# The last three tiles in front of a norm and the first three behind it, 256 tokens at a time

## The chip, the core and the metric

The kernel runs on one core of a Trainium2 chip. TensorE (PE) multiplies, the vector engine (DVE), the scalar engine (ACT) and GpSimd (POOL) do the elementwise work, SyncE (SP) issues most of the DMAs. Each engine works through its own queue in order and waits on semaphores. The metric is the device time of one execution in microseconds; lower is better.

## What is computed

Two layers over x of 512 tokens by 1024 channels, in float32. Each layer has a mixing part with three attention branches and an MLP, and both are wrapped in two norms:

```python
def rms_norm(x, g):
    return x * rsqrt(mean(x * x, -1) + EPS) * g

def hybrid_layer(x, ...):
    h = rms_norm(x, g_mix_pre)
    proj = h @ w_in          # latents, q, k, v of the branches, gate logits
    o_a, o_b, o_c = mla(...) @ w_o_mla, swa(...) @ w_o_swa, stick_breaking(...) @ w_o_sb
    mixed = gates[0] * o_a + gates[1] * o_b + gates[2] * o_c
    x = x + rms_norm(mixed @ w_out, g_mix_post)
    h = rms_norm(x, g_mlp_pre)
    u = square(relu(h @ w_up))                       # 4096 wide
    return x + rms_norm(u @ w_down, g_mlp_post)
```

## The kernel before

Everything is stored transposed: the 128 partitions are channels, the free axis is the 512 tokens, and x, h and y have 8 tiles of 128 channels each (`KT` = 8). A tile of a projection is one PSUM bank of 128 output channels by 512 tokens. It takes 24 matmuls: 8 blocks of the contraction, and for each three products (`three`, L470 to L476), because a float32 value a is split into `a_hi`, rounded to the matmul's type, and `a_lo`, the rest, and hi x hi, hi x lo and lo x hi are summed.

Weights come as chunks of 128 x 1024 through a ring of four slots (`RING`). SP waits until the chunk that held the slot has been used up and loads into `raw`; ACT rounds it to `w_hi` (`split`, L885 to L891), DVE subtracts to `w_lo` (`split`, L1372 to L1379). All orders are written out by hand, one program for each engine, and a table `ORDER` (from `order`, L32 on) names the tiles in the order in which PE makes them; semaphore counts are derived from it. Tiles take the two banks `proj` in turn.

A norm divides by a value that needs all 1024 channels of a token, so it sits between two rows of tiles. The one with gain `g_mix_post` (`POST`) comes behind the 8 tiles of the projection `out`; `MPOST` comes behind the 8 tiles `down` of the last of four groups (`GROUPS`) of the MLP. In what follows a joint is such a place: twice from `out` to `up`, once from `down` to the latents of the next layer, once from `down` to the output. At a joint, for all 512 tokens:

- ACT copies each `out` bank to y and squares it (L1301 to L1307); DVE gathers the squares into `acc` (`gather`, L1381 to L1393). For `down` DVE adds the bank to y first (L1688). PE sums over the partitions with two float32 matmuls against ones (`norm_sum`, L492 to L496), and then runs 28 matmuls whose result nobody reads (`keep_warm`, L499 to L502).
- ACT makes a first guess of the root with Ln and Exp (`norm_guess`, `guess`), DVE refines it with one Newton step in three instructions (`norm_refine`, `newton`).
- `residual` (L1415 to L1431) then runs over the 8 tiles on DVE: `hf` = y x gain x rstd, x += `hf`, and behind it `next_lo`; ACT makes `h_hi` = x x gain in between (`next_in`). The division of the following pre-norm is not waited for: it is applied later, to outputs, so h is x times its gain only.
- PE takes up h tile by tile: `three_tiles` (L528 to L542) keeps three output tiles open in three banks and adds each block of the contraction to all three when its `h_lo` is ready. It stands behind the joints and at the very start, there with weights that came in four pieces through the ACT queue (`first_low`, `first_high`).

At the start SP issues the vectors, x 0, the positions, a table of 16 columns `trig`, then x 1 to x 7; DVE begins with the angles of the positions and goes on to `w_lo` and `h_lo`.

## Time and profile before

| | |
|---|---|
| median of 3 runs | 1803.26 us (1802.73 to 1804.34) |
| the profiled execution | 1804.78 us, of which the span is 1803.0 us |
| granted TensorE clock, mean | 0.993 of full speed |
| busy shares of the span | PE 98%, DVE 59%, ACT 46%, POOL 8% |
| chain that ended last | PE 87%, DVE 7%, ACT 3%, issue 2%, DMA 1% |
| HBM read | 146.75 MB, 84 GB/s over the span |

The span runs from the first to the last event of the core; the rest of the profiled time lies around it. The busy share of an engine counts an instruction from its start to its end. Matmuls overlap one another, so their durations must not be added up; the distance from one start to the next is what a matmul costs. In the rows, "128x512" is partitions by elements, what stands behind "<-" in square brackets is the work that ended an idle time, and L475 is line 475 of the kernel.

### The profile page before, as it was taken

How to read it: one execution, taken by the hardware profiler on the slowest of the kernel's cores; microseconds unless marked ns; L12 is line 12 of the kernel's file. 1: busy time of each engine (PE TensorE's matmuls, PEld its weight loads, DVE VectorE, ACT ScalarE, POOL GpSimd, SP SyncE). 2: the span in 40 equal slices, each digit the busy share in tenths (PEclk: the TensorE clock that was granted, in tenths of full speed). 3: DMA queues.
4: the chain of work that ended last, by engine and by line, in shares of the span. 5: the costliest groups of instructions: out<-in, count | busy, mean ns of one | idle time of the engine just before them, and what ended most of it. 6: DMA issues, size and time to landing. Idle time of an engine off the chain costs nothing.

```text
span 1803.0 us, 20939 instructions
## 1 busy us (share of the span) xinstructions
PE 1760.2 (98%) x8298; PEld 1447.0 (80%) x8298; DVE 1057.7 (59%) x1378; ACT 827.0 (46%) x1115; POOL 145.5 (8%) x140
## 2 busy tenths in 40 slices
PE   8999999999999999999999999999999999999996
PEld 6888888888878888888778888888888788888884
DVE  6887875654547534354487777665544564344544
ACT  7576655555345413131366755655544353231221
POOL 0111121111100000000001112111111000000000
PEclk8999999999999999999999999999999999999998
DMA  4221112212332222222221221122224132222221
GB/s 149 65 69 67 60 60 70 71 66 75 123 100 90 92 94 99 94 93 94 93 99 62 74 71 48 59 71 71 71 86 138 57 117 94 93 94 94 99 93 66
DMA packets 46609, 152.30 MB, mean 84 GB/s; under 512 B 5296, under 2 KB 7728, under 8 KB 46512
## 3 DMA queue, kind: packets, MB, share of 16 engines
q1 hardware_dynamic: 44784, 147.29, 24.6%
q10 hardware_dynamic: 1728, 3.67, 0.5%
q8 instruction: 66, 1.08, 0.2%
...
HBM read 146.75 MB, written 4.19 MB: 84 GB/s over the span
## 4 chain that ended last, share of the span: by engine, by line
PE 87%; DVE 7%; ACT 3%; issue 2%; DMA 1%; POOL 0%; DVEq 0%; SPq 0%; ACTq 0%
PE bank L475 80%; PE bank L480 4%; PE bank L741 1%; PE bank L701 1%; DVE hf L1422 1%; DVE x L1429 1%; DVE w_lo L1378 1%; DVE h_lo L1411 1%; DMA trig<-in_trig 1%; ACT dn L943 0%; ACT dn L941 0%; ACT w_hi L891 0%; PE bank L551 0%; DVE mx L1472 0%; PE bank L496 0%
## 5 line engine op out<-in xcount | busy, mean ns | idle before, releaser
L475 PE MATMUL bank<-h_hi,w_hi 128*128 128x512 f32 x1248 | 492.2, 394 | 13.2 <-DVE h_lo L1411 11.6
L475 PE MATMUL bank<-h_hi,w_lo 128*128 128x512 f32 x1248 | 487.3, 391 | 0.0
L475 PE MATMUL bank<-h_lo,w_hi 128*128 128x512 f32 x1248 | 487.2, 390 | 0.0
L891 ACT ACTIVATE w_hi<-raw 128x1024 fp32r<-128x1024 f32 (+2 forms) x275 | 277.1, 1013 | 223.4 <-DMA raw<-in_w 222.8
L1378 DVE TENSOR_TENSOR w_lo<-raw,w_hi 128x1024 fp32r<-128x1024 f32 (+2 forms) x275 | 323.9, 1181 | 61.5 <-ACT w_hi L891 55.5
L475 PEld LDWEIGHTS bank<-h_hi,w_hi 128*128 128x128 f32 x1248 | 235.0, 188 | 66.9 <-issue 10.4
L475 PEld LDWEIGHTS bank<-h_hi,w_lo 128*128 128x128 f32 x1248 | 234.9, 188 | 49.8
L475 PEld LDWEIGHTS bank<-h_lo,w_hi 128*128 128x128 f32 x1248 | 235.1, 188 | 48.0 <-issue 1.4
L475 PE MATMUL bank<-u_hi,w_hi 128*128 128x512 f32 x512 | 203.0, 396 | 0.0
L475 PE MATMUL bank<-u_lo,w_hi 128*128 128x512 f32 x512 | 203.0, 396 | 0.0
L475 PE MATMUL bank<-u_hi,w_lo 128*128 128x512 f32 x512 | 203.0, 396 | 0.0
L1688 DVE TENSOR_TENSOR y<-bank,y 128x512 f32<-128x512 f32 x48 | 33.2, 692 | 142.5 <-PE bank L475 142.5
L475 PEld LDWEIGHTS bank<-u_hi,w_lo 128*128 128x128 f32 x512 | 96.4, 188 | 23.5
L475 PEld LDWEIGHTS bank<-u_lo,w_hi 128*128 128x128 f32 x512 | 96.4, 188 | 23.5
L475 PEld LDWEIGHTS bank<-u_hi,w_hi 128*128 128x128 f32 x512 | 96.4, 188 | 23.5
L1667 DVE TENSOR_TENSOR usq<-relu 128x512 f32<-128x512 f32 x64 | 44.3, 691 | 106.0 <-ACT relu L1090 105.4
L1090 ACT ACTIVATE relu<-bank 128x512 f32<-128x512 f32 x48 | 28.6, 595 | 139.2 <-PE bank L475 139.2
L475 PE MATMUL bank<-o_hi,w_hi 128*128 128x512 f32 x192 | 77.4, 403 | 0.0
L475 PE MATMUL bank<-o_hi,w_lo 128*128 128x512 f32 x192 | 76.1, 397 | 0.0
L475 PE MATMUL bank<-o_lo,w_hi 128*128 128x512 f32 x192 | 76.0, 396 | 0.0
L2019 POOL TENSOR_TENSOR mix<-mix,gate 128x512 f32<-128x512 f32 x32 | 44.4, 1391 | 367.8 <-DVE gate L1642 367.8
L1092 ACT ACTIVATE u_hi<-relu 128x512 fp32r<-128x512 f32 x64 | 40.5, 632 | 70.3 <-DVE relu L1662 68.8
...
## 6 DMA issues: line engine op xcount, KB each, us to landing
...
```

The costliest lines, as they stand in the source:

```text
L475: mm = pe.matmul(o, s, m, start=start and i == 0 and j == 0, stop=last and i == n - 1 and j == 2, skip_group_check=True)
L480: return pe.matmul(o, stationary, moving, start=False, stop=True, skip_group_check=True)
L701: mm = pe.matmul(to[:, off + col:off + col + w], a, m, start=off + col == 0 and i == 0, stop=i == 2, skip_group_check=True)
L741: mm = pe.matmul(pv_bank[:, q0:q0 + w], v[:, j, h % 2, :], part[:, s], start=i == 0 and part is p_hi, stop=part is p_lo, skip_group_check= ...
L891: act.activation(w_hi[:, gc % RING, 0:w], raw[:, gc % RING, 0:w], ACT.Copy).then_inc(whi.sem, 1)
L1090: act.activation(relu[:, n % 2, :], tile_bank(name)[:, :], ACT.Relu).then_inc(free_of(name), 1)
L1092: act.activation(u_hi[g % 2][:, t, :], relu[:, n % 2, :], ACT.Square).then_inc(u_h.sem, 1)
L1378: dve.tensor_tensor(w_lo[:, gc % RING, 0:w], raw[:, gc % RING, 0:w], w_hi[:, gc % RING, 0:w].bitcast(F32), ALU.subtract).then_inc(wlo.sem, 1)
L1411: dve.scalar_tensor_tensor(out=h_lo[:, t, :], in0=x[:, t, :], scalar=gain, in1=h_hi[:, t, :].bitcast(F32), op0=ALU.mult, op1=ALU.subtract) ...
L1667: dve.tensor_tensor(usq[:, n % 2, :], relu[:, n % 2, :], relu[:, n % 2, :], ALU.mult)\
L1688: ins = dve.tensor_tensor(y[:, t, :], tile_bank(name)[:, :], y[:, t, :], ALU.add)
L2019: pool.tensor_tensor(mix[:, t, :], mix[:, t, :], gated_at(b, t), ALU.add).then_inc(mix_add.sem, 1)
```

## The change

- `out` and the last group of `down`: tiles 0 to 4 (`HALF` = 5) stay whole. Tiles 5, 6, 7 are made for the first 256 tokens, then 5, 6, 7 again for the other 256 (`halved`). The first half's norm sum is placed in the middle of tile 5's second half, the second half's sum behind the first 9 matmuls of the three tiles that follow (`three_halves`). The second half of tile 7 gets a bank of its own (bank 4).
- The three tiles behind a joint run over all 8 blocks for the first 256 tokens, then for the other 256. `keep_warm` is gone from the joints.
- ACT squares an `out` bank where it lies and copies it to y with the gain applied; for `down` it scales y in place. `residual` therefore no longer multiplies by the gain, and works on two channel tiles of 256 tokens in one instruction. On DVE and ACT the second half's gathers, squares and guess stand between the pairs of the first half.
- The first two weight chunks behind a joint no longer pass through the ring but through two side buffers (`side_raw`, `side_hi`, `side_lo`) that lie over `o_lo` and a part of memory unused at that time.
- At the start positions and `trig` are issued from the ACT queue between the second and the third piece of the first weights; SP issues only the vectors and x before the ring. DVE makes two pieces of `w_lo` and two `h_lo` before it looks at the positions.
- SP stores the result in pairs of tiles, half the tokens at a time.

```diff
-WARM = 28
+HALF = 5
+ALL, HALF_A, HALF_B = slice(0, SEQ), slice(0, SEQ // 2), slice(SEQ // 2, SEQ)
+HALVES = (HALF_A, HALF_B)
...
+    def halved(*name):
+
+        return [e for t in range(HALF) for e in own(*name, t)] \
+            + [((*name, t, h), (*name, t)) for h in range(2) for t in range(HALF, KT)]
+
+    seq += halved("out")
...
-        seq += [e for t in range(KT) for e in own("down", g, t)]
+        seq += [e for t in range(KT) for e in own("down", g, t)] if g + 1 < GROUPS else halved("down", g)
...
+SIDE_CHUNKS = [l * CHUNKS + C[name] for l in range(DEPTH) for name in (("latent", 0), ("latent", 1), ("up", 0, 0), ("up", 0, 1))
+               if l or name[0] == "up"]
+FETCHED = []
+for gc in range(3, DEPTH * CHUNKS):
+    if gc not in SIDE_CHUNKS:
+        FETCHED.append(gc)
+    if gc + KT // 2 in SIDE_CHUNKS:
+        FETCHED.append(gc + KT // 2)
+IN_RING = [gc for gc in range(DEPTH * CHUNKS) if gc not in SIDE_CHUNKS]
+RING_AT = {gc: n for n, gc in enumerate(IN_RING)}
...
+        side_raw = place("side_raw", [P, 2, CH], F32, r1 + 8192)
+        side_lo = place("side_lo", [P, 2, CH], F32R, r1 + 8192)
+        side_hi = place("side_hi", [P, 2, CH], F32R, r1 + 24576)
...
                     sp.dma_start(x[:, t, :], A_x[:, t, :]).then_inc(x_loaded[t], 16)
-                    if t == 0:
-                        sp.dma_start(pos_i[:, :], A_pos.broadcast_to([P, SEQ])).then_inc(angles_loaded, 16)
-                        sp.dma_start(trig[:, :], A_trig).then_inc(angles_loaded, 16)
-                for gc in range(3, DEPTH * CHUNKS):
+                for gc in FETCHED:
                     c = gc % CHUNKS
                     if gc == RING:
                         sp.dma_start(cst_f[:, :], A_const).then_inc(const_loaded, 16)
-                    if gc >= RING:
-                        now[0] = (gc - RING) // CHUNKS
-                        sp.wait_ge(*full(LAST[(gc - RING) % CHUNKS] + 1))
+                    if gc in SIDE_CHUNKS:
+                        now[0] = gc // CHUNKS - (c < C["up", 0, 0])
+                        sp.wait_ge(*full(T[("o", 2, KT - 1) if c >= C["up", 0, 0] else ("down", GROUPS - 2, KT - 1)] + 1))
+                    elif gc >= RING:
+                        gone = IN_RING[RING_AT[gc] - RING]
+                        now[0] = gone // CHUNKS
+                        sp.wait_ge(*full(LAST[gone % CHUNKS] + 1))
...
+                def norm_sum(j, h=0):
+                    e, cols = square_of(j, KT - 1, h)
+                    pe.wait_ge(*summed(SUMMED_AT[j] + gathered(e - 1)))
+                    pe.matmul(sum_bank(h)[:, cols], cst[:, ONE, :].bitcast(F32), acc[:, cols], start=True, stop=False)
+                    pe.wait_ge(*squared(SQUARED_AT[j] + e + 1))
+                    pe.matmul(sum_bank(h)[:, cols], cst[:, ONE, :].bitcast(F32), sq[:, e % 2, cols], start=False, stop=True)\
                       .then_inc(sum_all.sem, 1)
...
+                def halved(name, hi, lo, j, ready=None):
+                    for t, h, one in tiles_of(*name):
+                        tile(one, hi, lo, ready if t == 0 else None,
+                             (lambda: norm_sum(j)) if (t, h) == (HALF, 1) else None, cols_of(t, h))
+                def three_halves(names, ready, j):
+                    def piece(name, t, h):
+                        cols = HALVES[h]
+                        return three(tile_bank(name)[:, cols],
+                                     [(weight(C[name], t), (h_hi[:, t, cols], h_lo[:, t, cols]))],
+                                     start=t == 0 and h == 0, last=t == KT - 1)
                     for name in names:
+                        pe.wait_ge(*wlo(C[name] + 1))
                         take_bank(name)
+                    for h in range(2):
+                        for t in range(KT):
+                            pe.wait_ge(*hlo(ready + KT * h + t + 1))
+                            for name in names:
+                                mm = piece(name, t, h)
+                                if h and t == KT - 1:
+                                    mm.then_inc(full.sem, 1)
+                            if (t, h) == (0, 0):
+                                layer = now[0]
+                                now[0] = layer - (j == MPOST)
+                                norm_sum(j, 1)
+                                now[0] = layer
...
-                    for t in range(KT):
-                        tile(("out", t), mix_hi, mix_lo, (mix_l, 0) if t == 0 else None)
-                    norm_sum(POST)
-                    keep_warm(WARM)
+                    halved(("out",), mix_hi, mix_lo, POST, (mix_l, 0))
 
...
-                    norm_sum(MPOST)
-                    if now[0] + 1 < DEPTH:
-                        keep_warm(WARM)
+                    if now[0] + 1 == DEPTH:
+                        norm_sum(MPOST, 1)
...
+                def out_part(t, h):
+                    name = ("out", t, h) if t >= HALF else ("out", t)
+                    cols = cols_of(t, h)
+                    tile_ready(name)
+                    square(POST, t, tile_bank(name), h)
+                    act.activation(y[:, t, cols], tile_bank(name)[:, cols], ACT.Copy, scale=vec(V_POST + t))\
+                       .then_inc(free_of(name), 1)
+
+                def down_part(t, h):
+                    act.wait_ge(*freed(("down", GROUPS - 1, t, h) if t >= HALF else ("down", GROUPS - 1, t)))
+                    cols = cols_of(t, h)
+                    square(MPOST, t, y[:, t, :], h)
+                    act.activation(y[:, t, cols], y[:, t, cols], ACT.Copy, scale=vec(V_MPOST + t))
...
                     act.dma_start(first(raw, i), A_first[:, 3 * P * a:3 * P * b])\
                        .then_inc(first_loaded[i], 16)
+                    if i == 1:
+                        act.dma_start(pos_i[:, :], A_pos.broadcast_to([P, SEQ])).then_inc(angles_loaded, 16)
+                        act.dma_start(trig[:, :], A_trig).then_inc(angles_loaded, 16)
...
-                        name = ("out", t)
-                        split(C[name] + 2)
-                        tile_ready(name)
-                        act.activation(y[:, t, :], tile_bank(name)[:, :], ACT.Copy).then_inc(free_of(name), 1)
-                        act.wait_ge(*freed(name))
-                        square(POST, t, y[:, t, :])
-                    split(C["up", 0, 2])
+                        if t < HALF:
+                            split(C["out", t] + 2)
+                        if t == HALF - 1:
+                            split(C["out", KT - 1])
+                        out_part(t, 0)
+                        if t == HALF - 1:
+                            split(C["up", 0, 0])
+                        elif t == HALF:
+                            split(C["up", 0, 1])
+                        elif t == HALF + 1:
+                            split(C["up", 0, 2])
                     norm_guess(POST)
+                    out_part(HALF, 1)
                     for t in range(KT):
-                        act.wait_ge(*res(t + 1))
-                        next_in(t, vec(V_MPRE + t))
+                        act.wait_ge(*res(t // 2 + 1))
+                        next_in(t, vec(V_MPRE + t), HALF_A)
+                        if t == 0:
+                            out_part(HALF + 1, 1)
+                        elif t == 3:
+                            out_part(HALF + 2, 1)
+                        elif t == 5:
+                            norm_guess(POST, 1)
...
+                def residual(p, h, n0, then):
+                    cols, n1, pairs = HALVES[h], n0 + KT // 2 * h, KT // 2
+                    def scaled_pair(q):
+                        if q > 1:
+                            dve.wait_ge(*res(n1 + q - 1))
+                        both = rstd[:, cols].unsqueeze(1).broadcast_to([P, 2, SEQ // 2])
+                        dve.tensor_tensor(hf[:, 0:2, HALVES[q % 2]], y[:, 2 * q:2 * q + 2, cols], both, ALU.mult)\
+                           .then_inc(scaled_y.sem, 1)
+                    def added_pair(q):
+                        dve.wait_ge(*scaled_y(n1 + q + 1))
+                        if n0 == 0:
+                            dve.wait_ge(x_loaded[2 * q], 16 * (now[0] + 2))
+                            dve.wait_ge(x_loaded[2 * q + 1], 16 * (now[0] + 2))
+                        to = x[:, 2 * q:2 * q + 2, cols]
+                        dve.tensor_tensor(to, to, hf[:, 0:2, HALVES[q % 2]], ALU.add).then_inc(res.sem, 1)
+                    if p == 0:
+                        scaled_pair(0)
+                        scaled_pair(1)
+                        added_pair(0)
+                        return
+                    if p < pairs:
+                        added_pair(p)
+                    if then:
+                        then(2 * p - 2, h)
+                    if p + 1 < pairs:
+                        scaled_pair(p + 1)
+                    if then:
+                        then(2 * p - 1, h)
...
-                angle_turns(3)
+                    next_lo(t, 2 * t + 2, vec(V_PRE + t, layer=0))
+
                 first_low(0)
                 x_low(0)
                 first_low(1)
                 x_low(1)
+                dve.wait_ge(angles_loaded, 2 * 16)
+                step(dve.tensor_copy(pos_f, pos_i[:, :]))
                 first_low(2)
                 x_low(2)
+                angle_turns(3)
+                x_low(3)
                 angle_less(3, parts[0:2])
-                x_low(3)
                 first_low(3)
...
+                    for p in range(KT // 2 + 1):
+                        residual(p, 0, 0, mlp_lo)
+                        if p == 0:
+                            gather(POST, HALF, 1)
+                        elif p == 1:
+                            gather(POST, HALF + 1, 1)
+                        elif p == 3:
+                            norm_refine(POST, 1)
```

On DVE, behind the last out tile of a layer: the norm's Newton step, then the residual (`hf`, x) and `h_lo`. Before:

```order
L1378 TENSOR_TENSOR w_lo<-raw,w_hi 128x1024 [waits w_hi_ready] x2
L1405 TENSOR_TENSOR rst<-rs_130 128x512 [waits rs_guess]
L1396 SCALAR_TENSOR_TENSOR rst<-rst,bank 128x512 [waits rs_square]
L1399 SCALAR_TENSOR_TENSOR rstd<-rst,rs_130 128x512 [waits rs_step]
L1422 SCALAR_TENSOR_TENSOR hf<-y,vec_all,rstd 128x512 [waits rs_step]
L1422 SCALAR_TENSOR_TENSOR hf<-y,vec_all,rstd 128x512
L1429 TENSOR_TENSOR x<-x,hf 128x512 [waits x_loaded0,scaled_y]
L1422 SCALAR_TENSOR_TENSOR hf<-y,vec_all,rstd 128x512
L1429 TENSOR_TENSOR x<-x,hf 128x512 [waits x_loaded1,scaled_y]
L1411 SCALAR_TENSOR_TENSOR h_lo<-x,vec_all,h_hi 128x512 [waits h_hi_ready]
```

After, at the same place:

```order
L1562 TENSOR_TENSOR rst<-rs_133 128x256 [waits rs_guess]
L1552 SCALAR_TENSOR_TENSOR rst<-rst,bank 128x256 [waits rs_square]
L1555 SCALAR_TENSOR_TENSOR rstd<-rst,rs_133 128x256 [waits rs_step]
L1580 TENSOR_TENSOR hf<-y,rstd 128x2x256 [waits rs_step]
L1580 TENSOR_TENSOR hf<-y,rstd 128x2x256
L1589 TENSOR_TENSOR x<-x,hf 128x2x256 [waits x_loaded1,x_loaded0,scaled_y]
L1549 TENSOR_TENSOR acc<-acc,sq 128x256 [waits summed,squared]
L1589 TENSOR_TENSOR x<-x,hf 128x2x256 [waits x_loaded3,x_loaded2,scaled_y]
L1568 SCALAR_TENSOR_TENSOR h_lo<-x,vec_all,h_hi 128x256 [waits h_hi_ready]
L1580 TENSOR_TENSOR hf<-y,rstd 128x2x256 [waits residual]
L1568 SCALAR_TENSOR_TENSOR h_lo<-x,vec_all,h_hi 128x256 [waits h_hi_ready]
L1549 TENSOR_TENSOR acc<-acc,sq 128x256 [waits summed,squared]
```

The rows of this chain are half as wide per tile or cover two tiles, and the gathers of the second half's squares (`acc`) now stand among them.

On PE, behind the last matmul of `out`: the sum, the filler and the first tiles of the MLP. Before:

```order
L475 MATMUL bank<-mix_hi,w_lo 128x512
L494 MATMUL bank<-acc,cst 128x512 [waits summed]
L496 MATMUL bank<-sq,cst 128x512 [waits squared]
L501 MATMUL bank<-cst 128x512 x28
L475 MATMUL bank<-h_hi,w_hi 128x512 [waits w_lo_ready,tile_free1,side_free,h_lo_ready,tile_free0]
L475 MATMUL bank<-h_lo,w_hi 128x512
L475 MATMUL bank<-h_hi,w_lo 128x512
```

After, from the ninth matmul behind `out` on (`side_hi` and `side_lo` are the side buffers' weights):

```order
L545 MATMUL bank<-h_hi,side_lo 128x256
L545 MATMUL bank<-h_hi,w_hi 128x256
L545 MATMUL bank<-h_lo,w_hi 128x256
L545 MATMUL bank<-h_hi,w_lo 128x256
L565 MATMUL bank<-acc,cst 128x256 [waits summed]
L567 MATMUL bank<-sq,cst 128x256 [waits squared]
L545 MATMUL bank<-h_hi,side_hi 128x256 [waits h_lo_ready]
L545 MATMUL bank<-h_lo,side_hi 128x256
L545 MATMUL bank<-h_hi,side_lo 128x256
```

The filler is gone, and what stands here is the second half's sum; the first half's has moved up into `out`.

On DVE at the start of the program. Before:

```order
L1702 TENSOR_SCALAR b_less<-vec_all 128x8
L1714 CAST tt_143<-pos_i 128x512 [waits angles_loaded]
L1350 TENSOR_SCALAR tt_144<-tt_143,trig 128x512 [waits setup_dve]
L1351 TENSOR_SCALAR tt_145<-tt_144 128x512 [waits setup_dve]
L1352 TENSOR_SCALAR tt_145<-tt_145 128x512 [waits setup_dve]
L1707 TENSOR_TENSOR w_lo<-raw,w_hi 128x384 [waits first_hi,setup_dve]
L1411 SCALAR_TENSOR_TENSOR h_lo<-x,vec_all,h_hi 128x512 [waits h_hi_ready]
```

After:

```order
L1877 TENSOR_SCALAR b_less<-vec_all 128x8
L1882 TENSOR_TENSOR w_lo<-raw,w_hi 128x384 [waits first_hi]
L1568 SCALAR_TENSOR_TENSOR h_lo<-x,vec_all,h_hi 128x512 [waits h_hi_ready]
L1882 TENSOR_TENSOR w_lo<-raw,w_hi 128x384 [waits first_hi]
L1568 SCALAR_TENSOR_TENSOR h_lo<-x,vec_all,h_hi 128x512 [waits h_hi_ready]
L1893 CAST tt_146<-pos_i 128x512 [waits angles_loaded]
L1882 TENSOR_TENSOR w_lo<-raw,w_hi 128x768 [waits first_hi,setup_dve]
L1568 SCALAR_TENSOR_TENSOR h_lo<-x,vec_all,h_hi 128x512 [waits h_hi_ready]
L1505 TENSOR_SCALAR tt_147<-tt_146,trig 128x512
```

The cast that waits for the positions has moved behind two `w_lo` and two `h_lo`.

## Rows read from the trace of the kernel before

**Rows 1.** The page, part 1: busy us, share and instructions of each engine.
```profile
PE 1760.2 (98%) x8298; PEld 1447.0 (80%) x8298; DVE 1057.7 (59%) x1378; ACT 827.0 (46%) x1115; POOL 145.5 (8%) x140
```

**Rows 2.** The waits of PE over the whole span: total us, times, longest.
```profile
PE bank L475 <- DVE h_lo L1411: 11.6, 7, 7.1
```

**Rows 3.** Timeline of PE, 528 to 557: start us, us, engine, line, instruction.
```profile
528.86 0.40 PE L475 MATMUL bank<-mix_hi,w_lo 128*128 128x512 f32 x1
529.10 1.02 PE L494 MATMUL bank<-acc,cst 128*128 128x512 f32 x2
...
539.34 0.47 PE L475 MATMUL bank<-h_hi,w_hi 128*128 128x512 f32 x1 [1.21 <-DVE h_lo L1411]
...
553.66 0.39 PE L475 MATMUL bank<-h_hi,w_hi 128*128 128x512 f32 x1
...
556.38 0.39 PE L475 MATMUL bank<-h_hi,w_hi 128*128 128x512 f32 x1
```

**Rows 4.** Timeline of ACT and DVE in the same norm.
```profile
531.77 0.60 ACT L908 ACTIVATE rs<-bank 128x512 f32<-128x512 f32 x1 [0.27 <-PE bank L496]
...
533.07 0.69 DVE L1405 TENSOR_TENSOR rst<-rs 128x512 f32<-128x512 f32 x1 [0.31 <-ACT rs L910]
...
535.24 1.42 DVE L1422 SCALAR_TENSOR_TENSOR hf<-y,vec_all,rstd 128x512 f32<-128x512 f32 x2
...
538.44 0.75 DVE L1411 SCALAR_TENSOR_TENSOR h_lo<-x,vec_all,h_hi 128x512 fp32r<-128x512 f32 x1
```

**Rows 5.** Timeline of PE at 190: the attention's matmuls of 256 and 128 columns.
```profile
190.02 0.28 PE L475 MATMUL bank<-bp_hi,wv_hi 128*128 128x256 f32 x1
...
190.97 0.28 PE L475 MATMUL bank<-bp_hi,wv_lo 128*128 128x256 f32 x1
...
191.15 0.28 PE L475 MATMUL bank<-bp_lo,wv_hi 128*128 128x128 f32 x1
191.26 0.27 PE L475 MATMUL bank<-bp_hi,wv_lo 128*128 128x128 f32 x1
```

**Rows 6.** Timeline of ACT: it reads two tiles of the out projection.
```profile
523.67 0.60 ACT L1305 ACTIVATE y<-bank 128x512 f32<-128x512 f32 x1 [3.41 <-PE bank L475]
...
529.30 0.60 ACT L1305 ACTIVATE y<-bank 128x512 f32<-128x512 f32 x1 [3.42 <-PE bank L475]
```

**Rows 7.** Timeline at 57 to 63: ACT and DVE on 256 columns, DVE strided.
```profile
57.01 0.40 ACT L891 ACTIVATE w_hi<-raw 128x256 fp32r<-128x256 f32 x1
...
58.13 0.41 DVE L1378 TENSOR_TENSOR w_lo<-raw,w_hi 128x256 fp32r<-128x256 f32 x1
...
62.51 0.68 DVE L1516 TENSOR_TENSOR mv_lo<-bank,mv_hi 128x512 fp32r<-128x512 f32 x1
```

**Rows 8.** Timeline of DVE at the start of layer 1.
```profile
918.86 2.28 DVE L1738 TENSOR_TENSOR xsq<-xsq 128x2048 f32<-128x2048 f32 x1
...
925.08 0.69 DVE L1745 TENSOR_TENSOR csq<-csq 128x512 f32<-128x512 f32 x1 [1.95 <-ACT csq L1144]
```

**Rows 9.** Timeline of the tail.
```profile
1783.97 1.02 PE L494 MATMUL bank<-acc,cst 128*128 128x512 f32 x2
...
1799.13 1.29 DVE L1429 TENSOR_TENSOR x<-x,hf 128x512 f32<-128x512 f32 x2
```

**Rows 10.** Timeline of the start, and last the window 12 to 14 (clock, DMA share).
```profile
11.55 0.43 DVE L1714 CAST tt<-pos_i 128x512 f32<-128x512 int32 x1 [7.93 <-DMA trig<-in_trig]
...
12.21 0.72 ACT L923 ACTIVATE h_hi<-x,vec_all 128x512 fp32r<-128x512 f32 x1 [5.60 <-DMA x<-in_x]
...
14.74 0.79 PE L475 MATMUL bank<-h_hi,w_hi 128*128 128x512 f32 x1 [7.08 <-DVE h_lo L1411]
...
16.77 1.47 ACT L1106 ACTIVATE w_hi<-raw 128x1536 fp32r<-128x1536 f32 x1
...
36.78 1.02 PE L484 MATMUL bank<-xsq,cst 128*128 128x512 f32 x2
...
12.00:14.00 2.00, 0.00 (x0) 0.00 (x0) 1.88 (x5) 1.79 (x4) 0.00 (x0) 0.50 1.06 405
```

318 lines of the change are left out of this document (195 added, 123 removed).

## The prediction

> **What bounds the kernel now.** I read the page first: TensorE is busy 98% of the span and the vector engine 59% [rows 1], so what can be won is time in which TensorE does nothing useful, and what can be lost is extra time in its queue. The list of waits names little: TensorE idles 11.6 us for `h_lo`, 7.1 of them in one piece at the start [rows 2]. That list is too kind, since the 28 filler matmuls behind each norm's sum count as busy. So I went to the timeline around the first norm behind the out projection [rows 3]. The last matmul of that projection starts at 528.86, the first of the MLP at 539.34, and the three tiles that take h as it comes end at 556.38. Of the 27.28 us from 529.10 to 556.38 the three tiles need 72 x 0.227 = 16.34; 10.94 us go to the norm. There are four such places: two of these, one between the layers, and the tail. What fills them is a serial chain [rows 4]: sums, Ln, Exp, three Newton steps, then per tile a scaled y, the add to x, h_hi and h_lo, each 512 tokens wide.
>
> **One caution on reading.** A 512-wide matmul is shown 0.39 us long, but they start 0.227 us apart ((556.38 - 553.66) / 12, [rows 3]), and in the out projection 0.234: ACT reads its tiles 5.63 us apart (529.30 - 523.67, [rows 6]), 24 matmuls each. Sums are made with start distances, not durations.
>
> **Edit 1, halves.** Three tiles in front of and three behind a norm become 256 columns wide: per joint 2 x 144 half matmuls for 2 x 72 whole ones. The nearest rows are the 256-wide ones of the banded attention [rows 5]: from 190.02 to 190.97 eight distances, 0.119 each. A 128-wide one is 0.11 from the next (191.15, 191.26), half the columns for nearly the same distance, so 0.11 looks like what a weight load needs, just under 0.119. The halves then cost 288 x 0.119 = 34.3 us per joint against 16.9 + 16.3 = 33.2: +1.1 us. Bounds: 0.115 to 0.125, -0.1 to +2.8 us; I take 0.119, the same width on the same line.
> The Trainium skill ("TensorE: Matmul & The Clock Gate", What overlaps and what doesn't) says that a weight load overlaps running matmuls only when its row group differs, which speaks against this change. By that rule the 0.11 of the load would stand bare in front of every stream, and no matmul of 256 columns could follow the last by 0.119, nor would four times the columns of a 128-wide one take only twice its distance; here the trace disagrees. What the change would cost if the rule held for the added loads is rival 1.
>
> **Edit 2, the joint out to MLP (twice).** Count from 0 = the start of tile 5, second half; the first halves of 5, 6 and 7 are done. PE needs 2.86 us per half tile. ACT squares tile 7's first half straight from the bank (0.40, [rows 7]) by 0.63, in time for the sum placed halfway in the tile, at 1.43. The sum is two fp32 matmuls of two passes each; two whole passes take 1.02 [rows 3], by my reading 0.43 from one to the next and 0.59 for the last. Halves are then 0.21 and 0.38: result at 1.43 + 3 x 0.21 + 0.38 = 2.45, PE's queue held 0.86. That half-width is an estimate, no row has it. Ln and Exp at 0.40 + 0.03 each: 3.35. Three half-wide DVE steps, 0.41 + 0.03 each [rows 7]: 4.7. Two pairs of scaled y (512 elements again, 0.69, issued 0.60 apart) and the first add: 6.6; one half gather, the second add, h_lo (0.48): h_lo 0 at 8.0. PE has work until 0.86 + 3 x 2.86 = 9.44. **The chain is hidden with 1.4 us to spare.** PE then meets the second sum behind the first nine matmuls, at 10.5; ACT has squared tile 7's second half at 10.05 (tile full at 9.64; on ACT it stands behind h_hi 0, tile 6's square and scaling, and h_hi 1 to 3, the last of them waiting for the add at 7.6 and done at 9.25). From there PE eats a pair of tiles in 18 x 0.119 = 2.14 us while DVE makes one in 0.60 + 0.60 + 2 x 0.39 = 1.98, with 0.7 for gathers and 1.3 for the second Newton in between: its last h_lo is at 22.9, PE wants it near 26. Nothing waits, except about 0.1 us for a bank at the end, which relu can read only 0.5 us before it, with 0.6 to read. After: 34.3 + 2 x 0.86 + 0.1 + small gaps 0.2 = 36.3. Before: 16.9 + 27.3 = 44.2. **7.9 us each, 15.8 together.** Low bound 5, if ACT or DVE comes 2 to 3 us late; high bound 9.
> The two weights that the halves need early (up 0 and 1) come through side buffers: their loads wait only for the last branch projection, tens of us earlier. The third goes into the slot of out 4, free 8.4 us before zero and needed at 9.4: 17.8 us of cover for a load and two splits of 1.05 and 1.22. Their cost is nil while those covers stand; if one lands late, PE stands by just that much.
>
> **Edit 3, the joint down to the next layer (once).** Same, but DVE must first add each bank to y, then ACT squares and scales. ACT gets to the square of tile 7's second half only after scaling tile 6 and two more h_hi: 12.6, where PE stands at 10.5. DVE shows it in the order too: two bank adds and a gather that waits for ACT stand between the pairs. The second sum is a wait that is new: 2.1 us. Also ACT squares x and issues the spill only in the second half; before, DVE's xsq sum began 4.3 us ahead of the end of the three tiles and still had 1.95 us idle behind it [rows 8]; now it ends about 3.4 behind, where PE asks at 2.7, and DVE enters the latents about 1 us late. I take 1.3. **7.9 - 2.1 - 1.3 = 4.5.** Bounds 1 to 7.
>
> **Edit 4, the last joint.** Behind the last three tiles comes no matmul, only the tail: 1783.97 to 1803.0 is 19.0 us [rows 9]. With halves the first half's residual runs beside tiles 6 and 7; the second sum is at 11.1, its Newton ends at 14.35, eight pair operations at 0.60 end at 19.25, and the stores take 2.6 (1800.42 to 1803.0). After: 8.6 + 21.85 = 30.4; before 16.9 + 19.0 = 35.9. **5.4.** Bounds 3.5 to 6.5.
>
> **Edit 5, the start.** PE's first real matmul is at 14.74, because DVE's first queue entry waits for positions and the small table (7.9 us of waiting, to 11.5) and because x 1 landed at 12.2 behind them on SP's queue [rows 10]. Now x is alone there, and DVE takes two pieces of w_lo and h_lo first: w_hi at 6.61, w_lo 7.2, h_lo 7.95, and PE starts near 8.0, 0.3 us after the warm-up. The granted clock is 0.50 from 12 to 14 us, the lower of its levels, 1.2 GHz, after PE had stood since the warm-up's end near 7.7; with real work from 8 on I expect the full level, 2.4 GHz. But pos and trig now stand ahead of the two large pieces of w on ACT's queue, so the later tiles are gated; piece 4 (768 KB) must land by 16.77, where ACT splits it now, or the term is lost. ACT's splitting of piece 4 (16.77 before) starts perhaps 2 us sooner, and everything of DVE behind it (its w_lo, the last h_lo and the angles, some 10 us, and the xsq sum, 4.3 us) moves with it: PE meets that sum near 32 instead of 36.78. **4.0.** Bounds -1 (pieces late) to 5.5.
> The Trainium skill ("DMA: Bandwidth & Descriptors", Issuing engines are not separate DMA queues) says that transfers issued from different engines run on the same 16 DMA engines. All that must land is the same, so by it only the order changes and the last landing does not; the DMA share of 1.06 from 12 to 14 us [rows 10], all engines at work, agrees. That would give rival 3.
>
> **Sum.** 15.8 + 4.5 + 5.4 + 4.0 = 29.7 us. The profiled run took 1804.78 with a span of 1803.0, so 1.8 lies outside; the span should be 1773.3 and the median 1803.26 - 29.7 = **1773.6**.
>
> **The rivals.**
> 1. Weight loads show, and it ends slower. A split adds a load: four sets of 72 in front and three behind, 504 more. If the second half's load is not hidden, each costs the 0.11 of [rows 5]: 55.4 us, time 1829. It decides from 29.7 / 504 = 0.059 us per split on, that is a 256-wide distance of about 0.148. Against it: eight distances in a row at 0.119, each with its own load. 3%.
> 2. DVE sets the pace of the joints. The pair operations read y with stride and a repeated rstd, which no row has exactly; 0.3 us more on each of the eight pairs' two operations is 4.8 per joint, of which the slack takes half: about 2.5 in three joints and 3 at the end, 1784; with the late second sum of edit 3 at all joints (2.1 more each) 1788. For it: margin of only 1.4. Against it: a strided write costs the same, 0.68 for 512 [rows 7]. 12%.
> 3. The start brings nothing, or costs 1: the pieces of w land together with the last x as before, ACT splits piece 4 at 16.8 again, and only the first tiles are early: 1777.6 to 1778.6. Inside the range; 20%.
> 4. The joints work, but the start's and the middle joint's gain is given back in the latents and the first heads, where DVE and not PE is last: 1803.3 - 15.8 - 5.4 - 2 = 1780. TensorE's waits there are small [rows 2], which speaks against it. In the range too; 10%.
> 5. The change takes more than I see, below 1766: 4%.
>
> **Numbers.** Forecast 1773.6; 1766 to 1783 holds 0.80: 0.50 for the main case, 0.20 for rival 3, 0.10 for rival 4, and the bounds of 0.119 (1008 halves by -0.004 or +0.006: 1769.6 to 1779.6) with them. 0.12 for rival 2 above 1783, 0.03 for rival 1, 0.04 below, 0.01 for no difference. About 0.2% is what a measurement of this kernel can tell from none. Faster 0.96, same 0.01, slower 0.03.
>
> **What would show it.** 256-wide h, mix and u matmuls 0.117 to 0.121 apart; no TensorE idle over 0.5 us at the joints out to MLP, one of about 2 us in front of the second sum at down to latents; first real matmul at 8 us; a tail from the last matmul of some 10 us instead of 19. Wrong, if halves are 0.14 or more apart, if PE waits for `h_lo` in the second half, or if the first weights of a joint land late.

## The result: 1777.1 us, 1.5% faster, 3.5 us above the forecast

The changed kernel takes 1777.06 us (median of 4 runs, 1775.92 to 1777.83) against 1803.78 (1802.73 to 1804.34) of the kernel before, run beside it. The ratio is 0.985, with a 95% interval of 0.9839 to 0.9862. The forecast was 1773.6, with a range of 1766 to 1783.

The profiled execution took 1775.92 us, its span is 1774.1. In spans the gain is 28.9 us, where the prediction had 29.7. In medians it is only 26.7, and that difference turned out to be the more instructive one.

First the page: busy shares, and the shares of the chain that ended last. Then the waits of PE (us in total, times, longest):

```profile
PE 1743.8 (98%) x8734; PEld 1460.2 (82%) x8734; DVE 1061.9 (60%) x1428; ACT 843.9 (48%) x1187; POOL 145.3 (8%) x140
PE 90%; DVE 5%; ACT 3%; issue 1%; DMA 1%; SPq 0%; POOL 0%; ACTq 0%; DVEq 0%
```

```profile
PE bank L545 <- DVE h_lo L1568: 5.6, 5, 2.2
PE bank L545 <- DVE of L1652: 4.4, 8, 1.3
...
PE bank L565 <- DVE acc L1549: 0.8, 1, 0.8
...
PE bank L554 <- DVE xsq L1917: 0.6, 1, 0.6
```

Against [rows 1] the busy share says nothing (98% both times): 436 more matmul instructions are shown busy for 16 us less. Against [rows 2] the wait for `h_lo` has shrunk from 11.6 to 5.6 us, also far less than the gain, because the filler of before never counted as waiting.

The joint from `out` to the MLP in layer 0, on PE's timeline (start us, us, engine, line, instruction), which answers to [rows 3]:

```profile
518.42 0.59 PE L565 MATMUL bank<-acc,cst 128*128 128x256 f32 x2
...
526.28 0.29 PE L545 MATMUL bank<-mix_hi,w_lo 128*128 128x256 f32 x1
526.41 0.28 PE L545 MATMUL bank<-h_hi,side_hi 128*128 128x256 f32 x1
...
527.48 0.59 PE L565 MATMUL bank<-acc,cst 128*128 128x256 f32 x2
...
528.15 0.47 PE L545 MATMUL bank<-h_hi,side_hi 128*128 128x256 f32 x1
528.46 0.28 PE L545 MATMUL bank<-h_lo,side_hi 128*128 128x256 f32 x1
...
544.22 0.28 PE L545 MATMUL bank<-h_hi,w_lo 128*128 128x256 f32 x1
544.57 0.47 PE L545 MATMUL bank<-h_hi,w_hi 128*128 128x512 f32 x1
```

No row between 518.42 and 544.57 has an idle time in brackets. The first h matmul follows the last of `out` at the usual distance, 0.13 us. Behind a sum's first matmul the next h matmul starts 0.67 us later (527.48 to 528.15) and the one behind that 0.31 (528.46) instead of 0.12, so a sum costs the queue 0.98 - 0.12 = 0.86 us. From 528.46 to 544.22, 133 distances take 15.76 us, 0.118 each. DVE runs ahead of all this: its first `h_lo` is done at 524.95 (524.47 + 0.48), 1.5 us before PE asks for it.

```profile
524.47 0.48 DVE L1568 SCALAR_TENSOR_TENSOR h_lo<-x,vec_all,h_hi 128x256 fp32r<-128x256 f32 x1
...
534.23 0.48 DVE L1568 SCALAR_TENSOR_TENSOR h_lo<-x,vec_all,h_hi 128x256 fp32r<-128x256 f32 x1
```

Where the 28.9 us of span came from, read by laying the same matmul of both traces side by side (start before, start after, what the distance between them had grown by):

| place | before | after | gain there | forecast |
|---|---|---|---|---|
| start, up to the first heads | 450.99 | 447.32 | 3.7 | 4.0 |
| joint `out` to MLP, layer 0 | 556.38 | 544.57 | 8.1 | 7.9 |
| joint `down` to latents | 952.55 | 935.66 | 5.1 | 4.5 |
| layer 1, behind the banded heads | 1339.13 | 1323.89 | **-1.6** | 0 |
| joint `out` to MLP, layer 1 | 1444.52 | 1421.14 | 8.1 | 7.9 |
| tail, to the end of the span | 1803.0 | 1774.1 | 5.5 | 5.4 |

The terms of the sum are right to within 0.6 us each. One row of the table wasn't in the sum at all.

### 1.5 us given back where nothing was changed

In layer 1, ahead of the last banded head's values, PE idles 1.27 us (1.26 in the kernel before). The timeline of before, then of after:

```profile
1134.69 0.36 PE L475 MATMUL bank<-bp_hi,wv_hi 128*128 128x256 f32 x1 [1.26 <-DVE of L1481]
...
1136.65 0.40 PE L475 MATMUL bank<-h_hi,w_lo 128*128 128x512 f32 x1
1136.88 0.40 PE L475 MATMUL bank<-h_hi,w_hi 128*128 128x512 f32 x1
```

```profile
1117.83 0.36 PE L545 MATMUL bank<-bp_hi,wv_hi 128*128 128x256 f32 x1 [1.27 <-DVE of L1652]
...
1120.84 0.63 PE L545 MATMUL bank<-h_hi,w_lo 128*128 128x512 f32 x1
1121.27 0.63 PE L545 MATMUL bank<-h_hi,w_hi 128*128 128x512 f32 x1
```

The same matmuls stand 0.24 us apart before and 0.43 after. The windows of PE (window, us, busy us and matmuls, granted clock, DMA share, GB/s) say why; first after, then before:

```profile
1118.00:1120.00 2.00, 2.00 (x13) 0.62 0.04 8
1120.00:1122.00 2.00, 2.00 (x6) 0.52 0.00 0
```

```profile
1134.00:1136.00 2.00, 1.30 (x11) 1.00 0.04 8
1136.00:1138.00 2.00, 2.00 (x12) 1.00 0.00 0
```

The granted clock was 0.50, that is 1.2 GHz, from 1118.4 to about 1121.8, and 1.54 us were lost. In layer 0 of the same execution the same two idle times (0.61 at 238.37, 1.27 at 242.47) brought no fall. So the work and the idle time ahead are equal, and the clock falls in one case and not in the others.

### The profile page after: what moved, and what is told of

Its sections match the earlier page's. It is cut to its first block, busy times and chain, and to the rows that moved or that the text cites. A ratio compares the mean times of both kernels' runs of the same rounds, so it can differ in the third digit from the quotient of the medians.

```text
span 1774.1 us, 21987 instructions
## 1 busy us (share of the span) xinstructions
PE 1743.8 (98%) x8734; PEld 1460.2 (82%) x8734; DVE 1061.9 (60%) x1428; ACT 843.9 (48%) x1187; POOL 145.3 (8%) x140
## 4 chain that ended last, share of the span: by engine, by line
PE 90%; DVE 5%; ACT 3%; issue 1%; DMA 1%; SPq 0%; POOL 0%; ACTq 0%; DVEq 0%
PE bank L545 83%; PE bank L550 4%; PE bank L839 1%; PE bank L799 1%; DVE w_lo L1533 1%; DMA x<-in_x 1%; DVE hf L1580 0%; DVE x L1589 0%; ACT dn L1048 0%; ACT dn L1046 0%; PE bank L649 0%; ACT w_hi L991 0%; DVE of L1652 0%; PE bank L554 0%; ACT h_hi L1027 0%
## 5 line engine op out<-in xcount | busy, mean ns | idle before, releaser
L545 PE MATMUL bank<-h_hi,w_hi 128*128 128x512 f32 (+1 forms) x1224 | 478.1, 391 | 6.2 <-DVE h_lo L1568 4.1
L545 PE MATMUL bank<-h_hi,w_lo 128*128 128x512 f32 (+1 forms) x1224 | 473.2, 387 | 0.0
L545 PE MATMUL bank<-h_lo,w_hi 128*128 128x512 f32 (+1 forms) x1224 | 473.0, 386 | 0.0
L545 PE MATMUL bank<-u_hi,w_hi 128*128 128x512 f32 (+1 forms) x560 | 211.4, 377 | 0.0
L545 PE MATMUL bank<-u_hi,w_lo 128*128 128x512 f32 (+1 forms) x560 | 211.0, 377 | 0.0
L545 PE MATMUL bank<-u_lo,w_hi 128*128 128x512 f32 (+1 forms) x560 | 211.0, 377 | 0.0
L545 PEld LDWEIGHTS bank<-u_lo,w_hi 128*128 128x128 f32 x560 | 105.6, 189 | 21.3
L545 PEld LDWEIGHTS bank<-u_hi,w_hi 128*128 128x128 f32 x560 | 105.6, 189 | 21.3
L545 PEld LDWEIGHTS bank<-u_hi,w_lo 128*128 128x128 f32 x560 | 105.6, 189 | 21.2
L1856 DVE TENSOR_TENSOR y<-bank,y 128x512 f32<-128x512 f32 x32 | 22.1, 692 | 104.5 <-PE bank L545 104.5
L2230 POOL TENSOR_TENSOR mix<-mix,gate 128x512 f32<-128x512 f32 x32 | 44.4, 1392 | 367.9 <-DVE gate L1813 367.9
```

The source lines that it names most:

```text
L545: mm = pe.matmul(o, s, m, start=start and i == 0 and j == 0, stop=last and i == n - 1 and j == 2, skip_group_check=True)
L1856: ins = dve.tensor_tensor(y[:, t, :], tile_bank(name)[:, :], y[:, t, :], ALU.add)
L2230: pool.tensor_tensor(mix[:, t, :], mix[:, t, :], gated_at(b, t), ALU.add).then_inc(mix_add.sem, 1)
```

## The experiments

Twelve runs: the changed kernel again, ten edits of it and one of the kernel before. Each stands beside runs of the kernel before, 1803.98 to 1804.40 in the three groups; the changed kernel itself was repeated in the second group. The first four ask where the gain lies and what the small idle times are worth.

**The start undone.** Positions and `trig` back on SP's queue, DVE's order as before:

```diff
+                    if t == 0:
+                        sp.dma_start(pos_i[:, :], A_pos.broadcast_to([P, SEQ])).then_inc(angles_loaded, 16)
+                        sp.dma_start(trig[:, :], A_trig).then_inc(angles_loaded, 16)
...
-                    if i == 1:
-                        act.dma_start(pos_i[:, :], A_pos.broadcast_to([P, SEQ])).then_inc(angles_loaded, 16)
-                        act.dma_start(trig[:, :], A_trig).then_inc(angles_loaded, 16)
```

> The changed kernel with the start of the kernel before: positions and the small table between x 0 and x 1 on SP's queue, and the vector engine's first entry waiting for them. My account: the start is worth the 3.7 us that the traces show at the end of the first attention stages (450.99 before, 447.32 after), so the median rises from 1777.1 to 1780.8 and the first real matmul is near 14.7 us again. Rival 3 (the start brings nothing, the 3.7 us come from elsewhere): 1777.1.

Measured: 1776.62 us (1776.37 to 1776.96). That is rival 3's number. But the trace shows the start's cost all the same, 3.1 us at the first sum over x squared (36.55 against 33.46) and 2.7 at the stick-breaking values of layer 0, and then 1.5 us back in layer 1, where this execution had no fall of the clock. The medians hide the start behind something else; which value is right was left to a later run.

**The filler left out of the kernel before.**

```diff
-WARM = 28
+WARM = 0
```

> The kernel before with its three groups of 28 filler matmuls left out (they compute nothing that is used). My account: the serial chain behind each norm's sum stays as long, TensorE stands idle in it instead of being shown busy, and at best nothing changes: 1803.8; if TensorE's granted clock is at its lower level behind the idle 10 us, the matmuls behind it take twice as long for as long as that holds, up to 3 us per place: 1803.8 to 1813. Rival (the change gained because it dropped 84 fillers of 0.227 us): 1784.7.

Measured: 1808.90 us (1806.55 to 1809.95), ratio 1.0024 (1.0013 to 1.0035): slightly slower. The chain is as long as it was. PE's timeline and its windows at the first joint:

```profile
529.01 1.13 PE L496 MATMUL bank<-sq,cst 128*128 128x512 f32 x2 [0.49 <-ACT sq L905]
537.72 0.77 PE L475 MATMUL bank<-h_hi,w_hi 128*128 128x512 f32 x1 [7.59 <-DVE h_lo L1411]
```

```profile
532.00:534.00 2.00, 0.00 (x0) 0.82 0.00 0
534.00:538.00 4.00, 0.28 (x1) 0.50 0.00 0
538.00:542.00 4.00, 4.00 (x10) 0.50 0.02 4
542.00:544.00 2.00, 2.00 (x7) 0.62 0.00 0
```

Behind 7.59 us of idle time the clock stays at 0.50 for nearly 6 us of real work (537.72 to about 543.5), which costs some 2 us at each of two joints and 0.8 at the third (a fourth fall, 1.5 us, came behind the banded heads of layer 1). The gain isn't that of the dropped filler; the filler was worth its place as long as the chain was bare. With the halves, real matmuls stand where it stood, and the timeline above has no idle time there.

**Another order at the middle joint and in the tail.** The list of waits names `h_lo` for the largest remaining idle time there. The timelines of PE and DVE (rows of DVE first) disagree:

```profile
884.62 0.48 DVE L1568 SCALAR_TENSOR_TENSOR h_lo<-x,vec_all,h_hi 128x256 fp32r<-128x256 f32 x1
...
886.02 0.41 DVE L1868 TENSOR_TENSOR y<-bank,y 128x256 f32<-128x256 f32 x1
```

```profile
884.99 0.28 PE L545 MATMUL bank<-u_hi,w_lo 128*128 128x256 f32 x1
886.75 0.36 PE L545 MATMUL bank<-h_hi,side_hi 128*128 128x256 f32 x1 [1.48 <-DVE h_lo L1568]
```

`h_lo` is done at 885.10. What ends 0.3 us ahead of 886.75 is DVE's read of tile 6's bank (886.02 + 0.41), and that bank is one of the three that the new tiles want. The edit, in short:

```diff
                         if p == 0:
-                            down_part(HALF, 1)
-                        elif p == 1:
-                            down_part(HALF + 1, 1)
-                            down_part(HALF + 2, 1)
+                            down_added(HALF, 1)
+                            down_added(HALF + 1, 1)
+                            gather(MPOST, HALF, 1)
...
                             if t == 1:
                                 down_part(HALF + 1, 1)
-                            elif t == 3:
                                 down_part(HALF + 2, 1)
...
-                            x_square(t)
+                            if t > 1:
+                                x_square(t - 2)
```

> The changed kernel with another order at the joint down to latents and at the tail: the vector engine adds the banks of tiles 5 and 6 (second half) to y ahead of the second residual pair, tile 7's directly behind the first h_lo, the scalar engine squares tile 7 before h_hi 2, and squares x two steps behind its h_hi. My account: TensorE's 1.48 us in front of the first h matmul there are a wait for a bank that the vector engine reads late (it reads tile 6 at 886.02, TensorE was done with it near 882), not for h_lo, which was done at 885.1; so 1.5 us go at that joint, 0.5 at the sum of x, 0.8 to 1.1 at the tail: 1774.3 (range 1773.5 to 1775.5). Rival: the wait is for the chain of h_lo, as the list of waits names it; the order of the banks changes nothing at the joint and only the tail gains: 1776.

Measured: 1772.62 us (1770.82 to 1773.51), ratio 0.9823, 1.7 us under what was expected and below its range. Part of this is the clock: the mean granted clock of its four executions was 0.996 to 0.998, that of the changed kernel 0.996 each time. PE's first h matmul now follows the last of `down` by 0.25 us instead of 1.76, though `h_lo` is done later than before (886.22), so the wait was for the bank, not for the chain:

```profile
886.11 0.28 PE L545 MATMUL bank<-u_hi,w_lo 128*128 128x256 f32 x1
886.36 0.36 PE L545 MATMUL bank<-h_hi,side_hi 128*128 128x256 f32 x1
```

This execution had its fall of the clock in layer 0 (0.50 from 242 to about 245.4 us, +1.5 us) and none in layer 1. The edit moves the bank reads and the square of tile 7 together; what either alone would bring isn't shown.

**Real work into the idle time.**

```diff
                     stick_scores(0)
-                    band_values(HEADS - 1)
                     tile(("stick_vt", 0), h_hi, h_lo)
+                    band_values(HEADS - 1)
```

> The changed kernel with one projection tile (24 matmuls of 512 columns) moved ahead of the last banded head's values, where TensorE idled 1.27 us in each layer, in layer 1 right before its granted clock fell to 0.50 for 3.4 us (matmuls 0.43 us apart instead of 0.227, 1.5 us lost). My account: the tile covers the idle time, 2.5 us in both layers, and with it the clock's fall in layer 1 may go: 1774.6, or 1773.1 without the fall. Rival: the values come 5.5 us later and the vector and scalar engines that wait for them pass the delay on: 1777 or more.

Measured: 1786.10 us (1785.13 to 1787.60), 9 to 10 us slower, as the rival had it and worse. PE's timeline in layer 0:

```profile
260.00 0.77 PE L545 MATMUL bank<-h_hi,w_hi 128*128 128x512 f32 x1 [5.33 <-DVE tmp L1614]
```

The 1.27 us are gone, but the values come later by the tile, DVE passes the delay on, and PE stands 5.33 us ahead of the next tile in each layer, where it had stood 0.41 at most. The clock then fell in both layers. An idle time of PE at the head of a serial chain isn't room for work: here it is the distance that the other engines need.

The next four were run side by side, to separate the start, the clock and the order.

**The changed kernel again.**

> The changed kernel itself, as the measure for the three kernels run beside it: 1777.1. If the lower clock behind the banded heads comes and goes from execution to execution, its times spread by 1.5 us or so, as 1775.9 to 1777.8 did.

Measured: 1776.45 us (1775.76 to 1777.65), spans 1774.0 to 1775.8. The profiled execution (1776.13) had the fall at the same place, 0.50 from 1120 to 1122.

**Filler into the 1.27 us.**

```diff
                     stick_scores(0)
+                    take_bank(("stick_vt", 0))
+                    for _ in range(5):
+                        pe.matmul(tile_bank(("stick_vt", 0))[:, :], cst[:, ONE, :], cst[:, 0:4, :], start=True, stop=True,
+                                  skip_group_check=True)
                     band_values(HEADS - 1)
```

> The changed kernel with five filler matmuls of 512 columns (1.13 us, computing nothing that is used) in the 1.27 us in which TensorE idles ahead of the last banded head's values, once in each layer. My account: TensorE's clock falls behind that idle time in one layer or both in most executions, 1.5 us each time; the fillers cost nothing, since they lie in idle time, and keep the clock at 1.00: 1777.1 less 1.5 to 2.5 is 1775.1 (range 1774.3 to 1776), with a narrower spread. Rival (the fall has nothing to do with the idle time, or the fillers hold up the queue): 1777.1 to 1779.

Measured: 1773.97 us (1773.70 to 1774.39), 2.5 under the changed kernel beside it and 0.3 under the expected range. The spread fell from 1.9 to 0.7 us. The next matmul starts at the same moment as ever (PE's timeline), and the windows show the full clock:

```profile
1116.52 1.43 PE L927 MATMUL bank<-cst 128*128 128x512 f32 x5
1117.85 0.36 PE L545 MATMUL bank<-bp_hi,wv_hi 128*128 128x256 f32 x1
```

```profile
1118.00:1120.00 2.00, 2.00 (x15) 1.00 0.03 8
1120.00:1122.00 2.00, 2.00 (x10) 1.00 0.00 0
```

From 21 us on nothing moves between this trace and the changed kernel's until this point, and 1.54 us are gained at it. (At the start this execution kept its full clock, where the changed kernel's was at 0.50 from 12.6 to 16.0 us; the h matmuls at 21.0 us stand level, so that fall cost nothing.) A gain of 2.5 in the median is more than one fall. The mean granted clock of every execution is on record: 0.996 in all eight of the changed kernel, 0.998 in all five with filler. The difference, 0.002 of 1774 us, is worth two stretches of 3.4 us at half clock. In the two profiled executions one of them is the harmless one at the start; in the others both may lie in the attention and cost 1.5 each. That would explain the 2.5 us, but isn't shown.

The Trainium skill ("TensorE: Matmul & The Clock Gate", A second HAM failure mode: psum-queue depth-cycling) tells of a kernel in which short idle times between groups of matmuls made the clock swing. The runs here agree, with 1.5 us for each fall in the attention, and add that the same idle time need not do it every time.

**Filler, with the start undone.** Both edits together.

> The same five fillers per layer, with the start of the kernel before. In the first look the old start cost 3.15 us of span up to the sum of x and 2.7 up to the first head of layer 1, then a fall of the clock that the changed kernel had in layer 1 did not come, 1.5 us; the medians were the same. My account: with the clock held by the fillers in both, the start shows in full: 2.7 above the kernel with fillers and the new start, 1777.8. Rival 3 (the start brings nothing in the end): equal to it, 1775.1.

Measured: 1776.52 us (1776.02 to 1776.53), so the start is worth 2.55 us, about as expected and well apart from rival 3. With the old start, PE's first real matmul:

```profile
14.25 0.79 PE L548 MATMUL bank<-h_hi,w_hi 128*128 128x512 f32 x1 [7.39 <-DVE h_lo L1572]
```

**Filler, with the other order of the joint.** Both edits together.

> The other order of the joint down to latents and of the tail, with the five fillers per layer. The order alone gave 1772.6 (1770.8 to 1773.5), its profiled execution with one fall of the clock, in layer 0. My account: both add up, 1770.8 (1770.0 to 1771.8). Rival (the fillers do nothing): 1772.6.

Measured: 1771.88 us (1771.63 to 1772.89), ratio to the kernel before 0.9823 (0.9810 to 0.9837). This is the lowest median seen, 4.6 us under the changed kernel beside it. But it misses the expected range by 0.1 us, and its ratio is that of the order alone, so the two edits don't add up: on top of the filler the order brings 2.1 us, on top of the order the filler brings no gain that the ratios show, only a spread of 1.3 instead of 2.7 us. One execution of the order alone took 1770.82, at a mean granted clock of 0.998. At the sum of x the trace is 2.05 us ahead of that with filler alone (906.97, no wait), at the end 2.5; 0.4 of both is there at 15 us already, ahead of anything that the order touches. Two small waits are left, 0.66 us for the first `h_lo` of the second half and 0.37 at the tail's last sum:

```profile
895.16 0.38 PE L545 MATMUL bank<-h_hi,side_hi 128*128 128x256 f32 x1 [0.66 <-DVE h_lo L1575]
```

```profile
1759.27 0.70 PE L567 MATMUL bank<-sq,cst 128*128 128x256 f32 x2 [0.37 <-ACT sq L1012]
```

The last four measure prices that the prediction rested on.

**Halves away from any norm.** In `tile`, for `up`:

```diff
-                        mm = three(tile_bank(name)[:, cols], [(weight(c, t), (hi[:, t, cols], lo[:, t, cols]))],
-                                   start=t == 0, last=t == KT - 1)
+                            for a in parts:
+                                part = slice(a, a + 256)
+                                mm = three(tile_bank(name)[:, part], [(weight(c, t), (hi[:, t, part], lo[:, t, part]))],
+                                           start=t == 0 and a == 0, last=t == KT - 1)
```

> The changed kernel with every remaining matmul of the up projection (58 tiles of 24, both layers) cut into two of 256 columns, so 1392 matmuls more, each with a weight load of its own and no change to what must be ready when. It measures the price of a split where no norm is near. My account: 0.118 apart instead of 0.227, so 0.009 per split, 12.5 us: 1789. Rival 1 (each added load stands bare in front of its stream, 0.11): 153 us, 1929. If halves cost nothing at all: 1776.5.

Measured: 1793.74 us (1792.61 to 1794.84), +17.3 where 12.5 had been expected, that is 0.012 per split. The distance in these tiles is 0.120, not the 0.118 of the joint:

```profile
559.74 0.28 PE L545 MATMUL bank<-h_hi,w_hi 128*128 128x256 f32 x1
...
562.98 0.28 PE L545 MATMUL bank<-h_hi,w_hi 128*128 128x256 f32 x1
```

27 distances take 3.24 us. Rival 1 would have decided from 0.059 per split on; the measured price is a fifth of that. The statement of the Trainium skill behind it ("TensorE: Matmul & The Clock Gate", What overlaps and what doesn't), that a load overlaps running matmuls only if its row group differs, is not what these rows show.

**Quarters.** The same edit with parts of 128, for `up` 1 alone.

> The changed kernel with the 16 tiles of one group of the up projection (up 1, both layers; 384 matmuls) cut into four of 128 columns each, 1152 matmuls more. My account: a matmul can't follow the last sooner than its weight load needs, 0.11, so four take 0.44 instead of 0.227 and the 384 cost 82 us: 1858. Rival (time goes by columns alone, 0.057 for 128): 1776.5 to 1780.

Measured: 1860.45 us (1860.20 to 1862.32), +84, expected 82. PE's timeline:

```profile
574.82 0.28 PE L545 MATMUL bank<-h_hi,w_hi 128*128 128x128 f32 x1
...
577.94 0.28 PE L545 MATMUL bank<-h_lo,w_hi 128*128 128x128 f32 x1
```

28 distances take 3.12 us, 0.111 each, for half the columns of a 0.120. So in a row of matmuls, each with a weight load of its own, halving the columns from 256 to 128 saves next to nothing. That the load sets these 0.11 us is likely, but no run leaves the load out. Nor does it hold for every pair: right ahead of the two matmuls from which the prediction read its 0.11 ([rows 5]), the kernel before has two of 128 columns 0.06 apart (191.09 and 191.15). The change stops splitting where splits are still nearly free.

**The scaled pair done twice.** Its result goes into a spare buffer the first time.

```diff
+                        spare = (rst2[:, 0, :] if q % 2 else hf[:, 2, :]).rearrange("p (a c) -> p a c", a=2)
+                        dve.tensor_tensor(spare, y[:, 2 * q:2 * q + 2, cols], both, ALU.mult)
                         dve.tensor_tensor(hf[:, 0:2, HALVES[q % 2]], y[:, 2 * q:2 * q + 2, cols], both, ALU.mult)\
```

> The changed kernel with each of the vector engine's pair operations y times rstd done twice, once into a buffer that nothing reads: 0.60 us more on each of the eight pairs of a joint, four joints. It measures how near the vector engine is to setting the pace (rival 2). My account: the slack of 1.4 us in front of the first h_lo takes the two operations there, the rest shows only as far as it goes beyond the 3 us that the last h_lo had to spare: 1 to 2 us at each of the two joints to the MLP, 3 at the joint to the latents, 3 to 4 at the tail, 1786 (range 1783 to 1789). If the vector engine has room everywhere but in the tail: 1779 to 1780. If it already sets the pace: 4.8 at each of the four, 1796.

Measured: 1791.64 us (1789.86 to 1792.63), +15.2 instead of +9.5. By the traces: 3.7 at each joint to the MLP, 3.6 at the latents (some 1.2 of it a fall of the clock between 894 and 898), 4.6 at the tail. The waits of PE in the joint of layer 0:

```profile
529.05 0.70 PE L565 MATMUL bank<-acc,cst 128*128 128x256 f32 x2 [0.51 <-DVE acc L1549]
539.28 0.39 PE L545 MATMUL bank<-h_hi,side_hi 128*128 128x256 f32 x1 [1.64 <-DVE h_lo L1568]
```

The point that decides isn't the last `h_lo`, by which the prediction measured the slack (3 us), but the first of the second half. In the changed kernel it is done at 534.71 (534.23 + 0.48, above), and PE asks for it near 535.8, 62 distances of 0.118 behind 528.46: 1.1 us of room. By then six of the eight doubled operations are done, 3.6 us.

**No side buffers for `up`.** Their chunks go through the ring, the splits stand later:

```diff
-SIDE_CHUNKS = [l * CHUNKS + C[name] for l in range(DEPTH) for name in (("latent", 0), ("latent", 1), ("up", 0, 0), ("up", 0, 1))
-               if l or name[0] == "up"]
+SIDE_CHUNKS = [l * CHUNKS + C[name] for l in range(1, DEPTH) for name in (("latent", 0), ("latent", 1))]
...
                         if t == 0:
                             out_part(HALF + 1, 1)
+                        elif t == 2:
+                            split(C["up", 0, 1])
...
+                        elif t == 4:
+                            split(C["up", 0, 2])
```

> The changed kernel without side buffers for the first two weights of the MLP: they go into the slots of out 4 and out 5 like all others, and the third into that of out 6, so that their loads wait for the second halves of these tiles, and their splits stand later on the scalar and vector engines, between h_hi and h_lo. (The side buffers of the next layer's latents stay.) My account: tile 6's second half ends 3.7 us before the first h matmul may start, a load takes 3.3 us and the two splits 2.3, so TensorE waits some 2 us for the third weight, and the vector engine, standing in front of its split, is late with the next h_lo: 2 to 5 us at each of two joints, 1780.5 to 1786.5. Rival (the loads had slack anyway, the side buffers buy nothing): 1776.5.

Measured: 1791.61 us (1789.73 to 1792.72), +15.2 where 4 to 10 had been expected; in the trace 7.2 at the joint of layer 0 and 7.0 at that of layer 1.

```profile
533.86 0.54 PE L544 MATMUL bank<-h_hi,w_hi 128*128 128x256 f32 x1 [4.95 <-DVE w_lo L1532]
```

PE stands 4.95 us for the third weight. Its load isn't all of it: DVE makes the second `w_lo` from 528.92 and the third from 532.27, straight behind an `h_lo`, so the splits stand in the queues too. Then the clock is at 0.50 to 0.68 (534 to 538 us), the rest of the 7.2. Without these side buffers 1 of the joint's 8.1 us would be left.

## Why the prediction was right, and what its last 3.5 us were

- **What bounds the kernel** held: the 10.9 us of the norm at the joint were a serial chain behind filler. Leaving out the filler alone cost 4.5 us in all; hiding the chain won 8.1 at each joint to the MLP.
- **Edit 1**, 0.119 per half: 0.118 in the joint, 0.120 in `up`. Rival 1 is refuted by 1392 splits at 0.012 each.
- **Edit 2**, 7.9 each: 8.1 each. From the start of tile 5 to the last of the three tiles the joint takes 36.0 us (508.56 to 544.57) for 36.3 forecast, and took 44.2 (512.22 to 556.38) for 44.2. A sum costs 0.86 us, as estimated; what is left is the distance, 0.118 for 0.119 over 288 halves, 0.3 us. The 1.4 us of slack ahead of the first `h_lo` was 1.5 (524.95 against 526.41). What was wrong is the statement that nothing else is near: the first `h_lo` of the second half has 1.1 us.
- **Edit 3**, 4.5: 5.1, with the waits in other places. The forecast let PE stand 2.1 us at the second sum, for the late square of tile 7. The square was as late as forecast, 12.7 us behind the start of tile 5's second half (875.72) for 12.6. But PE didn't reach the sum at 10.5:

```profile
887.88 0.59 PE L565 MATMUL bank<-acc,cst 128*128 128x256 f32 x2
888.44 0.70 PE L567 MATMUL bank<-sq,cst 128*128 128x256 f32 x2
888.79 0.47 PE L545 MATMUL bank<-h_hi,side_hi 128*128 128x256 f32 x1
```

```profile
887.99 0.40 ACT L1008 ACTIVATE sq<-y 128x256 f32<-128x256 f32 x1
```

  It reached it at 12.2 (887.88), having stood 1.48 us ahead of the first h matmul for tile 6's bank, and that wait covered most of the other: the sum cost 0.24 us more than its like in layer 0 (0.91 from 887.88 to 888.79, for 0.67). So 1.7 us were lost in two places, not 2.1 in one, and 0.57 followed at the sum of x (1.3 forecast). The step that failed is the one that puts PE at the second sum at 10.5: it left out that the new tiles want banks which DVE must first read. The order experiment shows that wait; it doesn't show the bank read and the square apart, since it moves both.
- **Edit 4**, 5.4 (its own figures give 35.9 - 30.4 = 5.5): 5.5, with 0.80 us of PE waiting for the last `acc` in it. Of the 0.8 to 1.1 us that the other order was to win there, some 0.5 came.
- **Edit 5**, 4.0: 3.7 in the traces, 2.55 when undone with the clock held. The first matmul started at 7.54, but the clock did not stay up: it was at 0.64 from 12 to 14 us and 0.50 from 14 to 16 (before 0.50 from 12 on), behind 2.22 us of waiting for x:

```profile
12.00:14.00 2.00, 1.91 (x5) 0.64 1.06 408
14.00:16.00 2.00, 2.00 (x6) 0.50 1.04 410
```

  This cost nothing in the end: with filler in layers 0 and 1, an execution started at 8.75 and kept 1.00 over the same windows, and at 21.0 us both stand level. Rival 3 had the right picture of the DMAs, all engines at work up to 16 us, and the wrong conclusion: the start is worth 2.55 us with all engines busy. That it is the first 9 matmuls and DVE's early pieces that win it is read from the traces, not tested one by one.
- **Rival 4** (gain given back in layer 1's attention) came true in size, 1.6 us, and not in kind: not DVE in the latents or first heads, but the clock behind the banded heads.
- **The sum** is 30.5 us where 29.7 were forecast, less 1.6 for the clock: 28.9. The forecast then took the difference of two profiled executions for that of two medians. The profiled one of before lies 1.0 us above its median, that of after 1.1 below. Together with the 0.8 us of the sum and with the kernel before, which took 1803.78 and not 1803.26 this time, these make the 3.5 us. With the clock held by ten fillers, the changed kernel has a median of 1773.97, 0.4 from the forecast and 30.0 under the kernel before. So the term that was missing is the granted clock behind 0.6 and 1.3 us of idle time, 2.5 us in the median. Why an execution has the fall or not stays open: the traces show equal idle times ahead of both.
